# Attention scores on two 64-row halves of the array instead of zero-padded query copies

## The chip, the cores and the metric
The kernel runs on one NeuronCore of a Trainium2 chip. The metric is the device time of one execution in microseconds (us); lower is better.

## The reference
One transformer layer over 1024 tokens of width 1024, all in fp32. Two groups of attention heads work side by side on one input projection; the scores `s` are what the change is about.

```
u = rmsnorm(h, attn_norm_g);  qa, ka, va, qb, kb, vb = split(u @ w_in)
# A: 8 query heads, 2 key/value heads, head width 64; a 64-token chunk of queries
#    reads its own chunk and the one before it (128 keys), with a sink and a T5 bias
s = einsum('bcqhgd,bckhd->bchgqk', qc, kb) / sqrt(64) + bias
m = maximum(max(s), sink);  e = exp(s - m);  w = e / (sum(e) + exp(sink - m));  oA = w @ v
# B: 4 heads, each with two query/key halves t=0,1 of width 64, value width 128
s = einsum('bqhtd,bkhtd->bhtqk', qb, k) / sqrt(64) + bias   # causal by chunks of 64
pr = softmax(s);  a = pr[t=0] - lam * pr[t=1];  oB = rmsnorm(a @ v) * 0.8
h = h + concat(oA, oB) @ w_out
h = h + relu(rmsnorm(h) @ w_up)**2 @ w_down
h = h + sigmoid(rmsnorm(h) @ w_gate) * (p @ w_ple)
y = rmsnorm(h)
```

## The kernel before
Activations lie transposed: features on the 128 partitions, 1024 tokens along the free axis. The large projections split each fp32 factor into a high and a low part and run three passes (`passes`, line 781; `wblock`, line 790). The order on each engine is written out by hand with semaphores.

The input projection makes 18 blocks of 128 features: two for A's keys and values (`KA`, `VA`), four for A's queries (`QA`), and per head of B one each for queries, keys and values (`QB`, `KB`, `VB`). A query block of A holds one query head of the first key/value head on partitions 0 to 63 and one of the second on 64 to 127 (`load_qa`, line 265); the one key block holds both key heads in the same way. A block of B holds t=0 on partitions 0 to 63 and t=1 on 64 to 127.

A score matmul contracts over 64 partitions only. The kernel before gives TensorE all 128: GpSimd copies the 64 rows of queries that count into `qs`, a buffer whose other 64 rows were set to zero once (line 396), and the matmul takes the whole key block as its moving operand. `stage_a` (line 412) makes these copies for A, `stage_b` (line 431) for B; `qs_ok` tells TensorE that they are there, and GpSimd waits on `a_s` before it overwrites one.

**Attention A** runs over eight tiles i of 128 queries. For each group g (one key/value head with its four query heads) TensorE does `score_a(i+1, g)`, `trans_a(i, g)` (transposes of the exponentials), `pv_a` (times the values) and, once a tile, `out_a` (`tile_a`, line 940). VectorE's `tile_a` (line 1326) does `den_a`, `soft_a` (adds the bias, takes the maximum), `norm_a` and `split_a`; ScalarE exponentiates (`exp_a`) and copies the transposes out (`evac_a`). The scores of the first tile are computed inside the block before last of the projection (`first_scores`, line 1021).

**Attention B** runs over 4 heads and, in each, 8 steps k. `ORDER = (0, 7, 1, 6, 2, 5, 3, 4)` gives the query block of a step: odd steps have long key ranges (1024, 896, 768, 640 columns), even steps short ones (128, 256, 384, 512). PSUM holds the scores of two steps. TensorE in step k (line 1003): `score_b(k+2, 0)`, `trans_b(k, 0)`, in steps 3 and 4 `out_b` of the previous head, `score_b(k+2, 1)`, a second round of `trans_b` where the range is over 512 columns, then `pv_b(k-1)`. `trans_b(k)` waits for `mix_b(k)`. VectorE in step k (line 1397): `soft_b(k+1, 1)`, in steps 3 and 4 `head_lo`, `soft_b(k+2, 0)`, `mix_b(k+1)`; `soft_b` adds the bias (L1353) and reduces to the maximum (L1356), `mix_b` joins the exponentials of the two halves (L1366, L1368, L1373) and waits for both. ScalarE in step k (line 655): `evac_b(k, 0)`, in steps 3 and 4 `head_hi` of the previous head, `exp_b(k+1, 1)`, a second `evac_b`, `take_b(k-1)`, `exp_b(k+2, 0)`.

Of the kernel before, what the change touches and what calls it, by code (L numbers as in the profile page):

```python
# [24 lines left out]
P = 128  # L25
T = 1024
# [53 lines left out]
def build(nc, x, p, attn_norm_g, w_in, rel_bias, sinks, lam_q1, lam_k1, lam_q2, lam_k2, subln_g, w_out,  # L80
          mlp_norm_g, w_up, w_down, ple_norm_g, w_gate, w_ple, final_norm_g, onehot, out):
    ctx = ExitStack()
    with ctx:
# [56 lines left out]
        qs = at("qs", [P, 8 * P], F32, a_qs)  # L140
# [38 lines left out]

        def s_at(k, t):  # L180

            return (2 + 2 * t) * 512 if k % 2 else t * 512
# [31 lines left out]
        qs_zero, qs_ok = sem("qs_zero"), sem("qs_ok")  # L214
# [39 lines left out]
        def _(sp):  # L254
# [30 lines left out]
            sp.dma_start(sink[:, :], sinks[0].partition_broadcast(P)).then_inc(misc_in, 16)  # L285
# [19 lines left out]
            for i in range(12):  # L305
                head = line_rows[i * P * LINE:(i + 1) * P * LINE - P].rearrange("(q l) -> q l", l=LINE - 1)
                head = head[:, P - 1:P - 1 + 256]
                dst = bias_a[:, i * 256:(i + 1) * 256] if i < 8 else bias_b[:, (i - 8) * 256:(i - 7) * 256]
# [53 lines left out]
        def _(pool):  # L362
# [32 lines left out]
            pool.wait_ge(x_ss, TT)  # L395
            nc.gpsimd.memset(qs[:, :], 0.0).then_inc(qs_zero, 1)
# [8 lines left out]
            pool.wait_ge(qs_zero, 1)  # L405
            nc.gpsimd.memset(ba[64:128, :, 0:128], NEG).then_inc(bias_ok, 1)
            pool.wait_ge(bias_ok, 4)
            pool.wait_ge(ps_free, QB)
            q3 = qkv[:, :].rearrange("p (j t) -> p j t", t=T)
            qs3 = qs[:, :].rearrange("p (j t) -> p j t", t=P)  # L410
# [12 lines left out]
            stage_a(0, more=False)  # L423
            pool.wait_ge(qs_ok, 2)
# [3 lines left out]
            with pool.Fori(1, TT) as i:  # L428
                stage_a(i)
# [18 lines left out]
            pool.wait_ge(a_s, 2 * TT)  # L448
            pool.wait_ge(ps_free, KB)
            for k in range(4):  # L450
                stage_b(0, k, reuse=False)
            for k in range(4, 8):
                stage_b(0, k)
            pool.wait_ge(qs_ok, AU + 2 * TT)
            for s in range(2):
                split_lo(OUT0 + s, s)
            with pool.Fori(0, B_HEADS - 1) as hh:
                for k in range(6):
                    stage_b(hh + 1, k)
                pool.wait_ge(qs_ok, AU + 2 * TT * (hh + 1) + 12)  # L460
                root_b(hh)
                for k in range(6, 8):
                    stage_b(hh + 1, k)
            pool.wait_ge(qs_ok, AU + 2 * TT * B_HEADS)
            root_b(B_HEADS - 1)
# [314 lines left out]
        def _(pe):  # L780
# [127 lines left out]
            def trans_a(i, g):  # L908
                pe.wait_ge(a_e, 2 * i + g + 1)
                if not (isinstance(i, int) and i == 0 and g == 0):  # L910
                    pe.wait_ge(a_at, 2 * i + g)
# [676 lines left out]
```

## Time and profile before
| | |
|---|---|
| runs | 1382.13, 1383.05, 1386.3 us; median 1383.05 |
| span of the profiled execution, first to last instruction | 1379.7 us |
| TensorE busy | 1333.9 us, 97% |
| VectorE busy | 442.2 us, 32% |
| ScalarE busy | 355.9 us, 26% |
| GpSimd busy | 477.8 us, 35% |
| mean granted TensorE clock | 0.994 |
| input projection | to about 240 us |
| attention A | about 240 to 313 us |
| attention B | about 313 to 457 us |
| output projection, MLP, gate, output | the rest |

The profile names engines PE (TensorE matmul), PEld (its weight loads, which overlap), DVE (VectorE), ACT (ScalarE), POOL (GpSimd) and SP or SPq (SyncE and its queue). "L970" is line 970 of the kernel. An fp32 matmul stands in it as two MATMUL and two LDWEIGHTS records, a transpose or a matmul of the split parts as one each. The end of a matmul is modelled, so records overlap; the time from start to start is what a record costs. All times count from the start of the span.

### The profile page before, as it was taken

The numbers are of one execution on the slowest core, as the hardware profiler recorded it, in microseconds if no ns is written. First come the engines' busy times: TensorE is split into PE (matmuls) and PEld (weight loads), VectorE is DVE, ScalarE is ACT, GpSimd is POOL, SyncE is SP. The second block draws the span as 40 slices with busy tenths as digits, with TensorE's granted clock in tenths as the row PEclk, the third lists the DMA queues.
The fourth block names the chain that finished last, engine by engine and source line by source line (L and its number), as shares of the span: only waits on it lengthen the run. The fifth ranks groups of instructions, "written<-read, shape, count | busy, mean of one in ns | idle before, by whom it ended". The sixth has DMA issues, their size and how long they took to land.

```text
span 1379.7 us, 17463 instructions
## 1 busy us (share of the span) xinstructions
PE 1333.9 (97%) x6285; PEld 1090.7 (79%) x6285; DVE 442.2 (32%) x598; ACT 355.9 (26%) x655; POOL 477.8 (35%) x293
## 2 busy tenths in 40 slices
PE   6999999998888899999999999999999999999997
PEld 5788888995555788888888888888888888888886
DVE  5510112887888232222111221122211122222324
ACT  7112101665666311121011110011100122113221
POOL 3121231112221377433223432234322334774743
PEclk9999999999999999999999999999999999999999
DMA  5433111001000312111111121111121111113203
GB/s 190 173 94 92 46 46 31 0 1 31 1 0 0 138 46 60 32 59 47 46 46 46 47 60 46 46 46 46 46 60 46 46 46 46 48 43 98 70 0 123
DMA packets 117872, 75.38 MB, mean 55 GB/s; under 512 B 12817, under 2 KB 115250, under 8 KB 117458
## 3 DMA queue, kind: packets, MB, share of 16 engines
q1 hardware_dynamic: 117554, 73.93, 17.3%
q10 hardware_dynamic: 288, 1.05, 0.2%
q8 instruction: 19, 0.31, 0.1%
q14 instruction: 11, 0.09, 0.0%
HBM read 64.22 MB, written 10.75 MB: 54 GB/s over the span
## 4 chain that ended last, share of the span: by engine, by line
PE 90%; DVE 3%; ACT 2%; issue 2%; DMA 0%; DVEq 0%; SPq 0%; ACTq 0%
PE ps L787 77%; PE ps L812 3%; PE ps L903 2%; PE ps L928 2%; PE ps L970 2%; ACT e_buf L627 1%; PE ps L990 1%; PE ps L980 1%; PE ps L916 1%; DVE e_buf L1373 1%; PE ps L871 1%; DMA x_raw<-in_x 0%; PE ps L820 0%; PE ps L1072 0%; DVE coef L1368 0%
## 5 line engine op out<-in xcount | busy, mean ns | idle before, releaser
L366 POOL TENSOR_TENSOR w_lo<-w_raw,w_hi 128x1024 fp32r<-128x1024 f32 x96 | 230.9, 2406 | 621.7 <-ACT w_hi L551 621.6
L787 PE MATMUL ps<-u_hi,w_hi 128*128 128x512 f32 x896 | 277.0, 390 | 0.0
L787 PE MATMUL ps<-u_lo,w_hi 128*128 128x512 f32 x896 | 276.1, 389 | 0.0
L787 PE MATMUL ps<-u_hi,w_lo 128*128 128x512 f32 x896 | 275.8, 389 | 0.0
L551 ACT CAST w_hi<-w_raw 128x1024 fp32r<-128x1024 f32 x98 | 103.3, 1054 | 651.9 <-PE ps L787 651.1
L787 PEld LDWEIGHTS ps<-u_hi,w_lo 128*128 128x128 f32 x896 | 168.2, 188 | 35.1
L787 PEld LDWEIGHTS ps<-u_lo,w_hi 128*128 128x128 f32 x896 | 168.2, 188 | 35.1
L787 PEld LDWEIGHTS ps<-u_hi,w_hi 128*128 128x128 f32 x896 | 167.4, 188 | 35.7 <-issue 1.6
L787 PE MATMUL ps<-z_hi,w_hi 128*128 128x512 f32 x624 | 193.4, 391 | 0.0
L787 PE MATMUL ps<-z_hi,w_lo 128*128 128x512 f32 x624 | 192.1, 389 | 0.0
L787 PE MATMUL ps<-z_lo,w_hi 128*128 128x512 f32 x624 | 192.1, 389 | 0.0
L1441 DVE TENSOR_TENSOR h<-ps,h 128x1024 f32 (+1 forms) x40 | 49.0, 1225 | 306.0 <-PE ps L787 306.0
L787 PEld LDWEIGHTS ps<-z_hi,w_hi 128*128 128x128 f32 x624 | 116.8, 188 | 25.3 <-issue 1.0
L787 PEld LDWEIGHTS ps<-z_lo,w_hi 128*128 128x128 f32 x624 | 117.1, 188 | 24.4
L787 PEld LDWEIGHTS ps<-z_hi,w_lo 128*128 128x128 f32 x624 | 117.1, 188 | 24.4
L1479 DVE TENSOR_TENSOR u_lo<-temp,u_hi 128x1024 f32 x32 | 39.2, 1226 | 173.2 <-ACT u_hi L703 170.0
L1476 DVE SCALAR_TENSOR_TENSOR temp<-ps,rstd 128x1024 f32<-128x1024 f32 x32 | 39.2, 1224 | 110.1 <-PE ps L787 106.5
L970 PE MATMUL ps<-qkv,qs 128*128 (+4 forms) x192 | 73.2, 494 | 0.0
L1246 DVE SCALAR_TENSOR_TENSOR qkv<-ps,rstd 128x1024 f32 (+1 forms) x18 | 22.0, 1225 | 152.9 <-PE ps L787 146.2
L703 ACT CAST u_hi<-temp 128x1024 f32 (+1 forms) x31 | 32.5, 1049 | 138.0 <-POOL temp L498 138.0
L473 POOL TENSOR_TENSOR sqt<-h 128x1024 f32 (+1 forms) x23 | 59.3, 2580 | 17.0 <-DVE h L1508 17.0
L498 POOL TENSOR_TENSOR temp<-temp 128x1024 f32<-128x1024 f32 x32 | 60.6, 1893 | 6.0 <-DVE temp L1476 6.0
(149 smaller groups left out, 1227.8 us busy)
## 6 DMA issues: line engine op xcount, KB each, us to landing
w_raw<-in_w_up SPq DMA_DIRECT2D x64, 256.0 KB, 3.0
w_raw<-in_w_down SPq DMA_DIRECT2D x64, 256.0 KB, 3.0
w_raw<-in_w_in SPq DMA_DIRECT2D x36, 256.0 KB, 3.2
x_raw<-in_x SPq DMA_DIRECT2D x8, 512.0 KB, 6.9
h_save<-h SPq DMA_DIRECT2D x1, 4096.0 KB, 11.1
w_raw<-in_w_out SPq DMA_DIRECT2D x16, 256.0 KB, 2.9
w_raw<-in_w_ple_gate SPq DMA_DIRECT2D x16, 256.0 KB, 3.0
out<-y_out SPq DMA_DIRECT2D x6, 512.0 KB, 5.1
```

Source lines behind the costliest of these rows:

```text
L366: nc.gpsimd.tensor_tensor(w_lo[:, s * D:(s + 1) * D], w_raw[:, s * D:(s + 1) * D], w_hi[:, s * D:(s + 1) * D].bitcast(F32), ALU.subtract). ...
L473: nc.gpsimd.tensor_tensor(sqt[:, :], hj, hj, ALU.mult).then_inc(sq_t, 1)
L498: nc.gpsimd.tensor_tensor(tj, tj, tj, ALU.mult).then_inc(z_sq, 1)
L551: nc.scalar.copy(w_hi[:, s * D:(s + 1) * D], w_raw[:, s * D:(s + 1) * D]).then_inc(hi_done, 1)
L703: nc.scalar.copy(u_hi[:, bass.ds((2 * i + s) * T, T)], temp[:, s * T:(s + 1) * T]).then_inc(z_hid, 1)
L787: mm = nc.tensor.matmul(o[i], w, xx[:, x0[i]], start=(first and n == 0), stop=(last and n == 2))
L812: mm = nc.tensor.matmul(bank(2 * s + half), w, xx[:, x0], start=(k == 0 and n == 0), stop=(k == DT - 1 and n == 2))
L903: mm = nc.tensor.matmul(ps[:, g * T + j * 256:g * T + (j + 1) * 256], qs[:, (4 * g + j) * P:(4 * g + j + 1) * P], qkv[:, bass.ds(KA * T + ...
L970: mm = nc.tensor.matmul(ps[:, s0:s0 + w], qs[:, q0:q0 + P], qkv[:, bass.ds((KB + hh) * T + c, w)], start=True, stop=True)
L1441: nc.vector.tensor_tensor(hj, bank(2 * s, 2), hj, ALU.add).then_inc(ps_free, 1)
L1476: nc.vector.scalar_tensor_tensor(out=tj, in0=bank(2 * s, 2), scalar=0.0, in1=rstd[:, :], op0=ALU.max, op1=ALU.mult).then_inc(ps_free, 1)
L1479: nc.vector.tensor_tensor(u_lo[:, bass.ds(j * T, T)], tj, u_hi[:, bass.ds(j * T, T)].bitcast(F32), ALU.subtract).then_inc(z_ok, 1)
```

## The change
The query copies go, with the buffer `qs`, the semaphores `qs_zero` and `qs_ok` and all of GpSimd's `stage_a` and `stage_b`. A score matmul now takes its 64 rows of queries and of keys straight from `qkv`, on partitions 0 to 63 or 64 to 127, so that the two matmuls of a pair use the two halves of the array's rows; they alternate in program order and write different PSUM banks.

In A a group g is now made of two query blocks with both their halves, in place of the four query heads of one key/value head. Sinks and biases are loaded in that order (`a_place`; four DMAs for the sinks in place of one), `pv_a` picks the value head by `j // 2`, and `out_a` puts the heads back in order.

In B `score_b` makes both halves in one call. It waits for the exponentials of both halves of step k-2, and in `step_b` it stands behind `trans_b(hh, k, 0)`, and ahead of `out_b`; before, t=0 stood in front of the transposes and t=1 behind `out_b`. In the last tile of A `score_b(0, 0)` for both halves stands where the t=1 half stood. On VectorE and ScalarE the order stays. TensorE's loops over tiles and heads are unrolled.

```
+        def a_place(head):
+
+            return 4 * (head % 4 // 2) + 2 * (head // 4) + head % 2
...
-            sp.dma_start(sink[:, :], sinks[0].partition_broadcast(P)).then_inc(misc_in, 16)
+            for c in range(4):
+                h0 = 4 * (c % 2) + 2 * (c // 2)
+                sp.dma_start(sink[:, 2 * c:2 * c + 2], sinks[0, h0:h0 + 2].partition_broadcast(P)).then_inc(misc_in, 16)
...
-            nc.gpsimd.memset(qs[:, :], 0.0).then_inc(qs_zero, 1)
...
-            def stage_a(i, more=True):
-
-                for g in range(2):
-                    if more:
-                        pool.wait_ge(a_s, 2 * i - 1 + g)
-                        pool.wait_ge(qs_ok, 2 * i + g)
-                    elif g:
-                        pool.wait_ge(qs_ok, 1)
-                    nc.gpsimd.tensor_copy(qs3[g * HD:(g + 1) * HD, 4 * g:4 * g + 4, :],
-                                          q3[g * HD:(g + 1) * HD, QA:QA + 4, bass.ds(i * P, P)]).then_inc(qs_ok, 1)
-
-            stage_a(0, more=False)
...
-            def stage_b(hh, k, reuse=True):
-
-                u = TT * hh + k
-                if reuse:
-                    pool.wait_ge(a_s, AU + 2 * (u - 4) + 2)
-                for t in range(2):
-                    pool.wait_ge(qs_ok, AU + 2 * u + t)
-                    nc.gpsimd.tensor_copy(qs3[t * HD:(t + 1) * HD, 4 * t + k % 4, :],
-                                          qkv[t * HD:(t + 1) * HD, bass.ds((QB + hh) * T + ORDER[k] * P, P)]
-                                          ).then_inc(qs_ok, 1)
-
...
             def score_a(i, g, k0):
-                pe.wait_ge(qs_ok, 2 * i + g + 1)
-                if not isinstance(i, int) or i > 0:
+                if i > 0:
                     pe.wait_ge(a_e, 2 * (i - 1) + g + 1)
-                for j in range(4):
-                    mm = nc.tensor.matmul(ps[:, g * T + j * 256:g * T + (j + 1) * 256],
-                                          qs[:, (4 * g + j) * P:(4 * g + j + 1) * P],
-                                          qkv[:, bass.ds(KA * T + k0, 256)], start=True, stop=True)
+                for j in range(2):
+                    for r in range(2):
+                        rows = slice(r * HD, (r + 1) * HD)
+                        q0, s0 = (QA + 2 * g + j) * T + i * P, g * T + r * HALF + j * 256
+                        mm = nc.tensor.matmul(ps[:, s0:s0 + 256], qkv[rows, q0:q0 + P],
+                                              qkv[rows, KA * T + k0:KA * T + k0 + 256], start=True, stop=True)
                 mm.then_inc(a_s, 1)
...
-                                              qkv[:, bass.ds(VA * T + k0 + kt * P + g * HD, HD)],
+                                              qkv[:, bass.ds(VA * T + k0 + kt * P + (j // 2) * HD, HD)],
...
-                    mm = nc.tensor.transpose(ps[:, 7 * 512 + j * P:7 * 512 + (j + 1) * P],
-                                             o_a[:, j * P:(j + 1) * P], ident[:, :])
+                    x0 = 7 * 512 + (2 * (j % 2) + j // 2) * P
+                    mm = nc.tensor.transpose(ps[:, x0:x0 + P], o_a[:, j * P:(j + 1) * P], ident[:, :])
...
                 for g in range(2):
                     if ahead:
                         score_a(i + 1, g, k1)
-                    else:
-                        score_b(0, 0, g)
+                    elif g:
+                        score_b(0, 0)
                     trans_a(i, g)
...
-            def score_b(hh, k, t):
+            def score_b(hh, k):
 
                 u = TT * hh + k
                 n = (ORDER[k] + 1) * P
-                pe.wait_ge(qs_ok, AU + 2 * u + t + 1)
-                if isinstance(hh, int) and hh == 0 and k < 2:
-                    pe.wait_ge(a_e, 2 * TT - 1 + k)
+                if u < 2:
+                    pe.wait_ge(a_e, 2 * TT)
                     if k:
                         pe.wait_ge(a_at, 2 * TT)
                 else:
-                    pe.wait_ge(a_e, AU + 2 * (u - 2) + t + 1)
+                    pe.wait_ge(a_e, AU + 2 * (u - 2) + 2)
                 for c in range(0, n, HALF):
                     w = min(HALF, n - c)
-                    q0, s0 = (4 * t + k % 4) * P, s_at(k, t) + c
-                    mm = nc.tensor.matmul(ps[:, s0:s0 + w], qs[:, q0:q0 + P],
-                                          qkv[:, bass.ds((KB + hh) * T + c, w)], start=True, stop=True)
-                mm.then_inc(a_s, 1)
+                    for t in range(2):
+                        rows = slice(t * HD, (t + 1) * HD)
+                        q0, k0, s0 = (QB + hh) * T + ORDER[k] * P, (KB + hh) * T + c, s_at(k, t) + c
+                        mm = nc.tensor.matmul(ps[:, s0:s0 + w], qkv[rows, q0:q0 + P], qkv[rows, k0:k0 + w],
+                                              start=True, stop=True)
+                        if c + w == n:
+                            mm.then_inc(a_s, 1)
...
             def step_b(hh, k, ahead=True, prev=None):
                 h2, k2 = (hh, k + 2) if k < 6 else (hh + 1, k - 6)
+                trans_b(hh, k, 0)
                 if ahead:
-                    score_b(h2, k2, 0)
-                trans_b(hh, k, 0)
+                    score_b(h2, k2)
                 if prev is not None and k >= 3:
                     pe.wait_ge(b_oc, TT * hh + k - 1)
                     out_b(prev, k - 3)
-                if ahead:
-                    score_b(h2, k2, 1)
                 if ROUNDS[k] == 2:
                     trans_b(hh, k, 1)
                 if prev is not None and k >= 3:
...
-            with pe.Fori(2, TT - 1) as i:
+            for i in range(2, TT - 1):
                 tile_a(i, (i - 2) * P, (i - 1) * P, i * P)
...
-            for t in range(2):
-                score_b(0, 1, t)
+            score_b(0, 1)
...
-            with pe.Fori(0, B_HEADS - 1) as hh:
+            for hh in range(B_HEADS - 1):
                 for k in range(SPLIT, TT):
```

## Rows read from the trace of the kernel before
**Rows 1.** The page's head: span, and each engine's busy time, share, instructions.

```profile
span 1379.7 us, 17463 instructions
PE 1333.9 (97%) x6285; PEld 1090.7 (79%) x6285; DVE 442.2 (32%) x598; ACT 355.9 (26%) x655; POOL 477.8 (35%) x293
```

**Rows 2.** Busy time by stretch, columns as in the header: A tile, B head.

```profile
254.21:263.42 9.21, 9.21 (x70) 8.70 (x70) 8.09 (x17) 6.07 (x21) 1.22 (x2) 1.00 0.00 0
349.85:385.00 35.15, 30.24 (x167) 20.39 (x166) 29.45 (x61) 23.92 (x70) 7.57 (x17) 1.00 0.00 0
```

**Rows 3.** Waits, 241 to 303 us: who for whom, us in total, times, longest.

```profile
DVE ps L1284 <- PE ps L903: 5.0, 8, 0.8
```

**Rows 4.** The chain that ended last: start us, length us, what.

```profile
217.18 3.45 PE ps L903 x16
...
265.16 1.78 PE ps L903 x8
...
380.99 1.72 PE ps L970 x4
```

**Rows 5.** Waits of one head of B, 349.85 to 385 us.

```profile
DVE rden L1366 <- ACT e_buf L627: 2.9, 3, 1.6
```

**Rows 6.** Timeline around the 32-row matmuls: start us, length us, what.

```profile
55.05 0.61 PE L787 MATMUL ps<-u_hi,w_lo 128*128 128x512 f32 x2
...
55.59 2.84 PE L871 MATMUL ps<-hotw,ones 32*128 32x384 f32 x8
...
58.36 0.72 PE L787 MATMUL ps<-u_hi,w_hi 128*128 128x512 f32 x2
```

**Rows 7.** Timeline, end of A, VectorE.

```profile
305.94 0.42 DVE L1305 TENSOR_TENSOR o_a<-ps,rden 128x256 f32<-128x256 f32 x1 [1.35 <-PE ps L928]
```

**Rows 8.** Timeline around k=7 of a head of B.

```profile
381.50 0.89 DVE L1373 SCALAR_TENSOR_TENSOR e_buf<-e_buf,coef 128x640 f32<-128x640 f32 x1
...
382.54 0.63 PE L980 MATMUL ps<-ident,e_buf 128*128 128x128 f32 x4
...
382.86 0.43 DVE L1353 TENSOR_TENSOR ps<-ps,bias_b 128x256 f32<-128x256 f32 x1
...
383.01 1.88 PE L970 MATMUL ps<-qkv,qs 128*128 x4
...
385.64 1.22 DVE L1356 TENSOR_REDUCE nmax<-ps 128x1 f32<-128x1024 f32 x1
...
387.86 1.14 ACT L627 ACTIVATE e_buf<-ps,nmax 128x1024 f32<-128x1024 f32 x1
...
389.21 0.17 DVE L1366 RECIPROCAL rden<-den_t 128x2 f32<-128x2 f32 x1 [1.55 <-ACT e_buf L627]
```

**Rows 9.** Timeline behind k=1.

```profile
355.94 0.65 PE L980 MATMUL ps<-ident,e_buf 128*128 128x128 f32 x4 [1.34 <-DVE e_buf L1373]
...
356.52 0.42 DVE L1353 TENSOR_TENSOR ps<-ps,bias_b 128x256 f32<-128x256 f32 x1
```

**Rows 10.** Timeline behind k=5, VectorE.

```profile
374.04 1.02 DVE L1373 SCALAR_TENSOR_TENSOR e_buf<-e_buf,coef 128x768 f32<-128x768 f32 x1
...
376.04 0.42 DVE L1353 TENSOR_TENSOR ps<-ps,bias_b 128x256 f32<-128x256 f32 x1
```

**Rows 11.** Timeline behind k=3, the previous head's output.

```profile
365.08 0.63 PE L999 MATMUL ps<-ident,o_n 128*128 128x128 f32 x4 [0.59 <-DVE o_n L1385]
...
366.71 0.75 DVE L1393 SCALAR_TENSOR_TENSOR u_lo<-ps,gb,u_hi 128x512 f32 x1 [0.84 <-ACT u_hi L652]
```

**Rows 12.** SyncE's DMA issues around its gap.

```profile
12.52 0.43 SPq L287 DMA_DIRECT2D lam_in<-in_lam_k  x1
...
18.52 4.32 SPq L263 DMA_DIRECT2D w_raw<-in_w_in  x4
```

**Rows 13.** Busy time and granted clock (the number behind POOL) by stretch.

```profile
308.90:310.60 1.70, 1.09 (x10) 0.98 (x10) 0.47 (x2) 0.00 (x0) 0.00 (x0) 1.00 0.00 0
...
312.30:314.00 1.70, 1.68 (x5) 1.25 (x6) 0.53 (x1) 0.00 (x0) 0.00 (x0) 0.50 0.00 0
```

More of the change, by code:

```diff
@@ L139, in build @@
         diag = at("diag", [P, TT * P], F32, a_rstd)
-        qs = at("qs", [P, 8 * P], F32, a_qs)
         def small(name, n, parts=P):
@@ L213, in build @@
         v_tr, v_cp = sem("v_tr"), sem("v_cp")
-        qs_zero, qs_ok = sem("qs_zero"), sem("qs_ok")
         a_s, a_m, a_e = sem("a_s"), sem("a_m"), sem("a_e")
@@ L307, in _ @@
                 head = head[:, P - 1:P - 1 + 256]
-                dst = bias_a[:, i * 256:(i + 1) * 256] if i < 8 else bias_b[:, (i - 8) * 256:(i - 7) * 256]
+                at_a = a_place(i) if i < 8 else 0
+                dst = bias_a[:, at_a * 256:(at_a + 1) * 256] if i < 8 else bias_b[:, (i - 8) * 256:(i - 7) * 256]
                 sp.dma_start(dst, head).then_inc(bias_in, 16)
@@ L393, in _ @@
                     split_lo(2 * i + s, s)
-            pool.wait_ge(x_ss, TT)
-            nc.gpsimd.memset(qs[:, :], 0.0).then_inc(qs_zero, 1)
             pool.wait_ge(bias_in, 12 * 16)
@@ L404, in _ @@
             pool.wait_ge(bias_ok, 3)
-            pool.wait_ge(qs_zero, 1)
             nc.gpsimd.memset(ba[64:128, :, 0:128], NEG).then_inc(bias_ok, 1)
             pool.wait_ge(bias_ok, 4)
-            pool.wait_ge(ps_free, QB)
-            q3 = qkv[:, :].rearrange("p (j t) -> p j t", t=T)
-            qs3 = qs[:, :].rearrange("p (j t) -> p j t", t=P)
-            def stage_a(i, more=True):
-                for g in range(2):
-                    if more:
-                        pool.wait_ge(a_s, 2 * i - 1 + g)
-                        pool.wait_ge(qs_ok, 2 * i + g)
-                    elif g:
-                        pool.wait_ge(qs_ok, 1)
-                    nc.gpsimd.tensor_copy(qs3[g * HD:(g + 1) * HD, 4 * g:4 * g + 4, :],
-                                          q3[g * HD:(g + 1) * HD, QA:QA + 4, bass.ds(i * P, P)]).then_inc(qs_ok, 1)
-            stage_a(0, more=False)
-            pool.wait_ge(qs_ok, 2)
             with pool.Fori(KB // 2, N_IN // 2) as i:
@@ L427, in _ @@
                     split_lo(2 * i + s, s)
-            with pool.Fori(1, TT) as i:
-                stage_a(i)
-            def stage_b(hh, k, reuse=True):
-                u = TT * hh + k
-                if reuse:
-                    pool.wait_ge(a_s, AU + 2 * (u - 4) + 2)
-                for t in range(2):
-                    pool.wait_ge(qs_ok, AU + 2 * u + t)
-                    nc.gpsimd.tensor_copy(qs3[t * HD:(t + 1) * HD, 4 * t + k % 4, :],
-                                          qkv[t * HD:(t + 1) * HD, bass.ds((QB + hh) * T + ORDER[k] * P, P)]
-                                          ).then_inc(qs_ok, 1)
             def root_b(hh):
@@ L446, in root_b @@
                 pool.wait_ge(b_rt, hh + 1)
[L448 to L454, printed above, removed]
             for s in range(2):
                 split_lo(OUT0 + s, s)
[L457 to L460, printed above, removed]
+            with pool.Fori(0, B_HEADS) as hh:
                 root_b(hh)
[L462 to L465, printed above, removed]
             def square(b, j, n, clears):
@@ L909, in trans_a @@
                 pe.wait_ge(a_e, 2 * i + g + 1)
-                if not (isinstance(i, int) and i == 0 and g == 0):
+                if i or g:
                     pe.wait_ge(a_at, 2 * i + g)
@@ L920, in pv_a @@
                 pe.wait_ge(a_at, 2 * i + g + 1)
-                if isinstance(i, int) and i == 0 and g == 0:
+                if i == 0 and g == 0:
                     pe.wait_ge(ps_free, N_IN)
@@ L1209, in _ @@
                 if t == 6:
-                    dve.wait_ge(misc_in, 7 * 16)
+                    dve.wait_ge(misc_in, 10 * 16)
                     l4 = lam_in[:, :].rearrange("p (a b d) -> p a b d", b=2, d=HD)
```

## Prediction, made before the changed kernel was run

> **What bounds the kernel now.** I began with the page [rows 1]: the span is 1379.7 us and TensorE is busy for 97% of it. Most of that is the projection and MLP blocks of line 787, which the change leaves alone. The score matmuls run only between 217 and 455 us, so the busy share of the whole says nothing here, and I asked next for the busy time in stretches of that part [rows 2]. In one tile of attention A (9.21 us) TensorE is busy throughout and VectorE for 8.09 us: TensorE is the bound, VectorE close behind. In one head of attention B (35.15 us) neither is full: TensorE 30.24 us, VectorE 29.45 us. There the order of the work decides, and the question for each edit is who waits for whom.
>
> The waits in A [rows 3] show VectorE waiting for the scores of line 903, 8 times, 5.0 us in total. That is all VectorE can win back. The chain of waits [rows 4] gives the price of the scores: each fp32 matmul leaves two records, and a record takes 3.45/16 = 0.216 us at 256 columns and 1.72/4 = 0.43 us at 512. In B the waits of VectorE [rows 5] go above all to the exponentials (2.9 us a head); none is for scores. Its idle time there is not caused by the length of a score matmul, since `score_b(k+2, 0)` was issued ahead of `trans_b(k, 0)`, in time in which TensorE waits for `mix_b(k)` anyway.
>
> **The change part by part.**
> *What a pair costs.* I take it that matmuls start in program order, that the two records of one matmul use the same half of the array and so follow each other, and that the first record for the other half may run beside the second. With a record D, two pairs of A then take 5 D instead of 8 D: 1.08 us instead of 1.73. In B the half t=0 is ready after as many records as before (its own), and t=1 one record later. No run here shows two halves side by side. The bounds are 4 D (full overlap) and 8 D (none); I take 5 D because the trace has the matmuls of a group strictly one behind the other at D [rows 4].
>
> The Trainium skill's "TensorE: Matmul & The Clock Gate" (Part 3, Packing small matmuls) has matmuls of different row groups starting some nanoseconds apart. Nothing in this trace shows it. By it a pair would take 2 D, and the result would be some 3 us lower than mine.
>
> *Going to a part of the array and back.* The nearest rows are the 32-row matmuls of line 871 [rows 6]. From the start of the first to the next full matmul lie 58.36 - 55.59 = 2.77 us for 8 records of 384 columns, where streaming at 0.43 x 384/512 = 0.32 us makes 2.58. The last full pair before starts at 55.05, 0.54 us ahead of the visit; its two records last 0.61 us with their tail and would be followed after an estimated 0.45. So a switch costs 0.1 us or so each way. Bounds: 0 and 0.3 us. It comes twice for every group of scores.
>
> Those rows show a small gap at each side of the visit. The Trainium skill's "TensorEngine Tiling (Array Packing)" (Tiling Modes, Key Properties) says that changing the mode drains the engine, which speaks against a change that alternates modes in each step; the trace agrees, at 0.1 us. Without it the sum would be 2.4 us smaller.
>
> *First scores.* 16 records of 0.216 become 9 of them plus two switches: 3.45 -> 1.94 + 0.2, -1.3 us. TensorE is busy before and after them, so all of it counts.
>
> *Tiles of A.* TensorE falls by 6 D = 1.3 us a tile and gains 4 switches (0.4): 9.2 -> 8.3 us. VectorE needs 9.21 less its wait, 8.5, and is next. So the gain is the 5.0 us of [rows 3], not the 7 that TensorE saves.
>
> *From A to B.* `score_b(0, 0)` now stands behind `pv_a(6, 1)` for both halves; VectorE wants its t=0 half ahead of `norm_a(6, 1)`, which it now starts at 305.94 [rows 7]. It waits for the scores (0.3) and adds and reduces them (0.6) first; 0.5 us of this is time that the next link waits for `trans_a` anyway. +0.4, between 0 and 0.9.
>
> *B: where the t=0 scores went.* Both halves now follow `trans_b(k, 0)`, which waits for `mix_b(k)`. VectorE's order is unchanged: after `mix_b(k)` it takes `soft_b(k+1, 1)`, then `soft_b(k+2, 0)`, then `mix_b(k+1)`. For odd k the next key range is long (1024, 896, 768, 640) and the work that covers it, `soft_b(k+1, 1)`, is short. Take k=7 [rows 8]: `mix_b` ends at 382.39, `trans_b` starts at 382.54 and the scores behind it at 383.01. The half t=0 (1024 columns, 4 records) is ready at 384.73, while VectorE began `soft_b` on it at 382.86, from scores made earlier. With 0.1 of hand-off it waits 1.95 us. Part comes back: the `mix_b` at 389.21 waited 1.55 us for exponentials that began at 387.86, though their `soft_b` was through at 385.64 + 1.22 = 386.86, because ScalarE's queue was behind. Now that `soft_b` is through at 388.8, the exponentials run from 388.95 for 1.35 us, and `mix_b` follows at 390.3 instead of 389.21. Net +1.1, 3 times.
> - k=1 (896 columns, records 2 x 0.43 + 2 x 0.32) [rows 9]: `trans_b` starts at 355.94, its scores 0.47 later, t=0 is ready at 357.9 plus 0.1; VectorE used it at 356.52. It waits 1.5 us and gets 0.3 back at the next exponential: +1.2 three times, +0.85 in head 0, 4.45 in all.
> - k=5 (640 columns, records 2 x 0.43 + 2 x 0.11) [rows 10]: `mix_b` ends at 375.06, and by the same steps the scores are ready 0.15 + 0.45 + 1.1 + 0.1 = 1.8 us later, where VectorE took them up at 376.04, after 1.0: +0.75, 4 times.
> - k=3 and k=4 with a previous head [rows 11]: `out_b` stood between the two halves, now behind both. For k=3 it goes from 365.08 to 366.1 (768 columns, the whole pair), for k=4 the full 3 D = 1.3 us comes ahead of it. VectorE's `head_lo` waits for `out_b` through ScalarE (366.71 against 365.08), so it slips by +1.0 and +1.3, 3 times each. In head 0 k=3 has no `out_b`, but its own late scores: +0.9.
> - Even k: the next range is short and `soft_b(k+1, 1)` long (1.2 us and more), so the scores are in time: 0.
>
> Sum: 3.3 + 4.45 + 3.0 + 3.0 + 3.9 + 0.9 = 18.55 us, and switches ahead of these 18 crossings (1.8) and behind the six with `out_b` (0.6): 21.0 us.
>
> *The rest.* GpSimd's copies into `qs` go: they were ahead of the scores, and no score waited for them. Three more DMA issues for `sink` fall in SyncE's gap from 12.95 to 18.52 us [rows 12], at 0.43 to 0.47 us each; if that gap were gone they would cost 1.4 us. The unrolled loops of TensorE cost nothing that a row shows: bounds -0.3 (fewer register operations, off the path) and +2 us (waiting for code, one long wait of this size); I take 0, as the unrolled head 0 runs like the looped ones.
>
> **Sum.** -1.3 - 5.0 + 0.4 + 21.0 = +15.1 us. Against the profiled execution's span this is 1394.8. The median of the runs, 1383.05, lies 3.35 us above that span, for what is outside the first and last instruction, so I predict 1383.05 + 15 = 1398 us.
>
> **The rivals.**
> - *TensorE bounds B as well, and the shorter scores pay.* For: it is the busiest engine and 90% of the chain that ended last. Against: [rows 5]. A head would save D for the four short ranges (1.1 us) and 0.43 + 2 D' for the long ones, D' being the second record (3.85): 4.9 us, 19.7 in four heads, with 5.9 in A: -25.6, 1357 us. It decides if VectorE's next instruction after `soft_b(k+1, 1)` does not wait for the scores, or if later waits give the delay back in full.
> - *No overlap (the change doesn't do what it says).* A saves nothing; t=0 is ready two records later in 15 crossings (0.86 each) and `out_b` one record later in three: 12.9 + 1.3. 15.1 + 5.9 + 14.2 = +35, 1418 us. For: fp32 matmuls of the same group never overlap now. Against: here the rows used are disjoint.
> - *The clock falls.* TensorE's granted clock was 1.00 all through B, but it fell to 0.50 (1.2 of 2.4 GHz) at 312.3 us, where shortly before it had been busy for 1.09 of 1.70 us [rows 13]. With the change B has TensorE busy about 60% of the time. About 9 us a head of transposes and scores lie on the path; at half clock for a third of B this is +12: 1410 us.
> - *The delays are mostly absorbed.* If ScalarE's and TensorE's slack returns more than I traced, B costs half, 10 us: 1387 us.
>
> **How the numbers follow.** Forecast 0.55, no overlap 0.10, clock 0.12, absorbed 0.10, TensorE bound 0.13. The range 1384 to 1418 takes in all but the TensorE-bound case and some tail: the low end is B at half cost with full overlap, the high end the case without overlap. A measurement here can tell about 0.3%, 4 us, from no change. Faster 0.14, same 0.08, slower 0.78.
>
> **What would show it.** In the new trace: VectorE's `soft_b` adds waiting 1 to 2 us for TensorE's scores behind odd k, about four times a head; a head lasting 40 us; a tile of A 8.5 us with VectorE full; first scores 2 us. A head under 35 us would make the order argument wrong; scores of 1024 columns lasting 3.4 us for both halves would mean no overlap; a granted clock below 0.9 in B would be the third rival.

## The result: 1408.8 us, and the profile of the changed kernel

| | before | changed |
|---|---|---|
| runs | 1382.1 to 1386.3 us | 1404.16, 1405.36, 1412.31, 1412.56 us |
| median | 1383.2 us | 1408.8 us |
| ratio of times | | 1.018 (95%: 1.015 to 1.021) |
| profiled run, its span | span 1379.7 us | 1412.31 us, span 1410.5 us |

The changed kernel is 1.8% slower; 1398 us was forecast, and the median lies inside the range of 1384 to 1418. Its runs fall in two pairs, and the mean granted clock goes with them: 0.978 in the two of 1404 and 1405 us, 0.970 in the two of 1412 us.

The head of the page, to be held against [rows 1]:

```profile
span 1410.5 us, 16954 instructions
PE 1332.0 (94%) x6285; PEld 1080.7 (77%) x6285; DVE 441.9 (31%) x598; ACT 355.6 (25%) x655; POOL 445.4 (32%) x212
...
PEclk8999999999788799999999999999999999999999
```

TensorE's busy time has hardly moved (1333.9 to 1332.0 us) though its score matmuls got shorter: a lower clock has stretched others. The row of the clock has its dip in slices 11 to 14 (353 to 494 us), which are most of attention B and a few us behind it.

I cut both profiled executions at the same places: the first record of the first scores, of A, of B, and of the output projection.

| stretch, us | before | changed | difference | forecast |
|---|---|---|---|---|
| up to the first scores | 217.2 | 218.8 | +1.6 | 0 |
| first scores to A | 22.35 | 21.17 | -1.2 | -1.3 |
| A with the hand-over to B | 73.7 | 68.1 | -5.6 | -4.6 |
| B | 143.8 | 178.3 | +34.5 | +21.0 |
| the rest | 922.6 | 924.2 | +1.5 | 0 |
| span | 1379.7 | 1410.5 | +30.8 | +15.1 |

The 1.6 us ahead of the first scores are not the change's doing: in the profiled executions of the experiments this stretch took 216 to 219 us, and 217 us in experiment 1, whose code is the same up to there.

Busy time by stretch of the changed kernel: all of A, all of B, one tile of A, one head of B, and the stretch behind the first scores of B. The columns are the stretch, its length, then busy time and instructions of PE, PEld, DVE, ACT and POOL, then the granted clock and DMA.

```profile
239.97:308.04 68.07, 64.77 (x534) 56.55 (x533) 59.58 (x123) 43.88 (x146) 0.00 (x0) 1.00 0.00 1
308.04:486.33 178.29, 122.57 (x646) 80.53 (x645) 116.77 (x234) 95.78 (x273) 9.78 (x5) 0.83 0.04 13
247.99:256.43 8.44, 8.44 (x73) 7.56 (x72) 8.02 (x18) 7.31 (x28) 0.00 (x0) 1.00 0.01 2
411.64:456.71 45.07, 31.90 (x164) 20.93 (x164) 29.56 (x61) 24.03 (x71) 1.64 (x1) 0.81 0.00 1
312.00:316.00 4.00, 1.60 (x5) 0.69 (x5) 3.45 (x9) 3.16 (x8) 0.00 (x0) 0.51 0.00 0
```

A tile of A takes 8.44 us against 9.21 [rows 2]. In the head of B VectorE's work is the same as before (29.56 us) and the head is 10 us longer, with a granted clock of 0.81 where before it was 1.00.

The waits of the whole attention part, 217 to 490 us (engine and line that wait, for whom, us in total, times, longest):

```profile
PE ps L940 <- DVE e_buf L1330: 41.1, 27, 3.0
...
DVE ps L1310 <- PE ps L929: 31.6, 16, 3.7
...
DVE u_lo L1350 <- ACT u_hi L609: 16.4, 6, 3.7
```

Line 929 is the score matmul of B, line 1310 VectorE's first add on scores (`soft_b`), line 940 the transposes, line 1350 `head_lo`. Before, VectorE waited in B mostly for exponentials [rows 5], and for scores once in all of B, 1.4 us; now it waits for scores 15 times in B and once (2.3 us) at the end of A. TensorE's waits for `mix_b` were 16.6 us in 17 times before and are 41.1 us in 27 now. The chain of waits shows the shorter pairs, to be held against [rows 4]; the `x8` row of line 929 is a whole pair of 1024 columns:

```profile
218.80 1.93 PE ps L862 x16
...
391.97 1.97 PE ps L929 x8
```

And the timeline behind k=7, the counterpart of [rows 8]:

```profile
391.32 0.66 PE L940 MATMUL ps<-ident,e_buf 128*128 128x128 f32 x4 [0.97 <-DVE e_buf L1330]
...
391.90 1.99 PE L929 MATMUL ps<-qkv 64*128 64x512 f32 x8
...
394.03 0.43 DVE L1310 TENSOR_TENSOR ps<-ps,bias_b 128x256 f32<-128x256 f32 x1 [2.23 <-PE ps L929]
```

The transposes wait for `mix_b` (e_buf, L1330), the scores stand behind them, and VectorE is idle for 2.23 us before its add; 1.95 us was forecast.

So the order theory has its mark in the trace, but B lost 13.5 us more than that theory forecast. Two things were to be told apart: the new places of the scores, and TensorE's clock.

### The profile page after: what moved, and what is told of

The parts are those of the page before. It is cut to its first block, busy times and chain, and to the rows that moved or that the text cites. A ratio compares the mean times of both kernels' runs of the same rounds, so it can differ in the third digit from the quotient of the medians.

```text
span 1410.5 us, 16954 instructions
## 1 busy us (share of the span) xinstructions
PE 1332.0 (94%) x6285; PEld 1080.7 (77%) x6285; DVE 441.9 (31%) x598; ACT 355.6 (25%) x655; POOL 445.4 (32%) x212
## 4 chain that ended last, share of the span: by engine, by line
PE 87%; DVE 7%; issue 2%; ACT 1%; DMA 1%; SPq 0%; DVEq 0%; ACTq 0%
PE ps L744 75%; PE ps L929 3%; PE ps L769 2%; PE ps L950 1%; PE ps L940 1%; DVE e_buf L1330 1%; DVE kmax L1244 1%; DVE ps L1241 1%; ACT e_buf L584 1%; DMA x_raw<-in_x 1%; DVE ps L1310 1%; PE ps L828 1%; DVE nmax L1313 0%; DVE coef L1325 0%; PE ps L959 0%
## 5 line engine op out<-in xcount | busy, mean ns | idle before, releaser
L744 PEld LDWEIGHTS ps<-u_hi,w_lo 128*128 128x128 f32 x896 | 169.0, 189 | 35.4
L940 PE MATMUL ps<-ident,e_buf 128*128 128x128 f32 x144 | 30.0, 326 | 45.0 <-DVE e_buf L1330 41.1
L940 PEld LDWEIGHTS ps<-ident,e_buf 128*128 128x128 f32 x144 | 18.6, 162 | 58.7 <-DVE e_buf L1330 46.8
```

What stands on the lines that cost most here:

```text
L744: mm = nc.tensor.matmul(o[i], w, xx[:, x0[i]], start=(first and n == 0), stop=(last and n == 2))
L940: mm = nc.tensor.transpose(ps[:, o:o + P], e_buf[:, e:e + P], ident[:, :])
```

## The experiments

All medians below stand against runs of the kernel before on the same chip (medians 1381.9 to 1383.2 us). The granted clock of B and B's length are from each kernel's own profiled execution.

### 1. Only the order put back: the pair ahead of the transposes

```
             def step_b(hh, k, ahead=True, prev=None):
-                trans_b(hh, k, 0)
                 if ahead:
                     score_b(h2, k2)
+                trans_b(hh, k, 0)
```

> The changed kernel with one edit: in each step of B both halves of score_b(k+2) stand ahead of trans_b(k, 0) instead of behind it. Order theory (the loss in B is VectorE waiting for the late t=0 scores and the late out_b): these waits go, B returns to the 144 us it had before or a little less, A keeps its 7 us; 1373 to 1382 us, and VectorE's adds of line 1310 wait under 5 us in all instead of 31.6. Rival, 64-row matmuls or the switches between array modes are what costs: the time stays above 1395 us. Rival, the clock: if TensorE's clock falls because 64-row matmuls count for less, it still falls here and the time lies between, near 1390 us.

Measured: 1380.9 us, ratio 1.0003 (0.998 to 1.003). One line moved gives back 28 us. B takes 145.7 us at a clock of 0.95 (the changed kernel's 178.3 at 0.83), so the 28 us are the order and what the clock lost with it. VectorE's waits for scores fall from 31.6 us to 5.6 (under 5 was expected), and the longest of them is at the end of A:

```profile
DVE ps L1310 <- PE ps L929: 5.6, 7, 2.8
```

Two middle heads read:

```profile
356.80:391.22 34.42, 25.66 (x166) 17.19 (x164) 29.36 (x61) 23.71 (x70) 1.64 (x1) 1.00 0.00 0
391.22:427.24 36.02, 27.27 (x166) 18.35 (x164) 29.47 (x61) 23.71 (x70) 1.64 (x1) 0.95 0.00 0
```

At full clock a head is 0.7 us shorter than before (35.15 [rows 2]), though TensorE has 4.6 us less to do in it: shorter scores are worth little in B. The next head has the same work at a clock of 0.95 and takes 1.6 us longer, so what was won goes again.

### 2. Only the places, without 64-row matmuls

The kernel before, with both calls moved to where the changed kernel has its pair.

```
+                trans_b(hh, k, 0)
                 if ahead:
                     score_b(h2, k2, 0)
-                trans_b(hh, k, 0)
+                    score_b(h2, k2, 1)
                 if prev is not None and k >= 3:
                     pe.wait_ge(b_oc, TT * hh + k - 1)
                     out_b(prev, k - 3)
-                if ahead:
-                    score_b(h2, k2, 1)
```

> The kernel before, zero-padded copies and all 128 rows, with one edit: both score_b calls of a step of B stand behind trans_b(k, 0) and ahead of out_b, as in the changed kernel. Order theory: B loses what the changed kernel lost there and some more, as the pair takes 8 D instead of 5 D ahead of out_b; A is as before: 1405 to 1418 us. Rivals (64 rows, mode switches): 1383 to 1388 us, no change.

Measured: 1418.0 us, ratio 1.026 (1.023 to 1.029). B takes 179.2 us, 35.4 more than before, with the padded copies and full-height matmuls all in place:

```profile
313.26:492.49 179.23, 131.29 (x646) 89.63 (x645) 117.62 (x234) 94.22 (x273) 32.17 (x59) 0.94 0.04 12
```

The places alone slow B down; the halves of the array are not needed for that. VectorE now waits for the padded scores too (300 to 490 us), and no wait of TensorE for GpSimd's copies shows there:

```profile
DVE ps L1352 <- PE ps L970: 23.4, 14, 3.2
```

The clock here is 0.94, so a part of the 35 us is clock too.

### 3. Only the halves, in the old places

The changed kernel, with `score_b(hh, k, t)` one half at a time where the kernel before had it (also at the end of A).

```
+                if ahead:
+                    score_b(h2, k2, 0)
                 trans_b(hh, k, 0)
-                if ahead:
-                    score_b(h2, k2)
                 if prev is not None and k >= 3:
                     pe.wait_ge(b_oc, TT * hh + k - 1)
                     out_b(prev, k - 3)
+                if ahead:
+                    score_b(h2, k2, 1)
```

> The changed kernel with the halves taken from 64 rows, but each score_b in its old place in B (t=0 ahead of the transposes, t=1 behind out_b, also at the end of A), so that pairs do not overlap in B and the array changes its mode twice as often. Order theory: B as before, A as in the changed kernel; 1375 to 1380 us. Mode-switch rival: two more switches a step, 32 steps, at 0.1 us or more each on the path: 1385 us or more. 64-row rival: above 1395 us.

Measured: 1388.9 us, ratio 1.005 (1.003 to 1.007); a miss, 9 us over the upper end of the order theory; the rival of the mode switches, 1385 us or more, had it right. A middle head:

```profile
368.81:405.34 36.53, 34.57 (x165) 20.89 (x164) 29.54 (x62) 23.93 (x72) 1.64 (x1) 1.00 0.00 0
```

At the same full clock a head is 1.4 us longer than before and TensorE is busy 4.3 us more, in 16 visits to one half of the array: 0.27 us a visit. Unpaired, they pay for going there and back and save nothing. All of B takes 159.5 us, TensorE is busy for 146.1 of them, a larger share than before, and yet the clock is 0.91; that was the first sign that the busy share alone doesn't tell the clock. The two middle heads both ran at 1.00, so the 1.4 us a head are not clock; the low stretches lie in the first head (0.51 from 318 to 335 us) and at the end of B.

### 4. The pair on one half: is there overlap?

```
                     for t in range(2):
-                        rows = slice(t * HD, (t + 1) * HD)
+                        rows = slice(0, HD)
```

and the same in `score_a`.

> The changed kernel with both matmuls of every pair on rows 0 to 63 (the scores of the second half are then computed from the first half's queries and keys, so that part of the result is left out). If the two halves of the array really run side by side, this takes it away: 16 first-score records take 3.45 us instead of 1.93, a tile of A 9.2 us instead of 8.4, long ranges of B are ready 0.5 to 0.9 us later: 1420 to 1430 us. If nothing overlapped, the time stays at 1405 to 1412 us.

Measured: 1462.8 us, ratio 1.058 (1.055 to 1.061). The size was missed by over 30 us. The first scores:

```profile
216.79 3.65 PE ps L862 x16
```

3.65 us against 1.93 for the same 16 records on alternating halves, whose streaming alone would be 3.45 one behind the other and 1.73 side by side: they do overlap, and fully. B takes 215.6 us, and this is why the size was missed:

```profile
318.42:534.03 215.61, 178.80 (x646) 110.43 (x645) 116.88 (x234) 95.36 (x273) 9.79 (x5) 0.73 0.03 8
```

TensorE is busy for 83% of B, about as in the kernel before (120.6 of 143.8 us, 84%, clock 0.99), and is granted 0.73. The two shares are not quite alike: at a lower clock the same matmuls stay busy longer, so a part of the 83% comes from the low clock itself.

### 5 and 6. Holding the clock: an idle matmul ahead of each wait for `mix_b`

```
+                pe.wait_ge(a_at, AU + HEAD_ROUNDS * hh + BEFORE[k] + r)
+                if r == 0:
+                    nc.tensor.matmul(ps[:, 6 * 512:6 * 512 + 512], ident[:, :], qkv[:, KA * T:KA * T + 512],
+                                     start=True, stop=True)
                 pe.wait_ge(b_a, TT * hh + k + 1)
-                pe.wait_ge(a_at, AU + HEAD_ROUNDS * hh + BEFORE[k] + r)
```

This adds work to the changed kernel (32 matmuls whose result nobody reads); to free their PSUM bank, the wait for `a_at` moves ahead of the wait for `mix_b`, which is alike in both kernels. In the second kernel they use rows 0 to 63 only (`ident[0:64, :]`, `qkv[0:64, ...]`), with the same columns.

> The changed kernel plus one idle matmul in each step of B: 128 rows, 512 fp32 columns into the transposes' bank, while TensorE waits for mix_b ahead of trans_b(k, 0); its result is overwritten. 32 of them, 0.86 us each, 27.5 us of extra TensorE work, part of it past the end of the wait. Clock theory (beyond the 20 us of the late scores, B loses some 5 to 15 us because the granted clock falls to 0.8): the clock in B rises above 0.93 and the time falls in spite of the extra work, to 1395 to 1403 us. Rival, order alone: the clock is no cause, the extra work costs where it overruns, 1409 to 1425 us.

> The same with the idle matmul on 64 of the 128 rows. If TensorE's clock is held up by the matmuls' being there, this does as well as the 128-row one, within 3 us. If 64-row matmuls hold the clock up less, the granted clock in B stays nearer to the changed kernel's 0.83 and the time lies 4 us or more above that of the 128-row one.

Measured: 1399.2 us (ratio 1.011, 1.008 to 1.013) with all 128 rows, 1410.8 us (1.020, 1.018 to 1.023) with 64. B, first with 128 rows and below it a head of it:

```profile
309.84:476.20 166.36, 135.47 (x709) 77.99 (x709) 116.67 (x234) 96.24 (x273) 9.78 (x5) 0.97 0.04 10
409.94:450.27 40.33, 32.80 (x180) 19.07 (x180) 29.54 (x61) 24.15 (x71) 1.64 (x1) 1.00 0.00 0
```

and with 64 rows:

```profile
309.60:485.15 175.55, 148.56 (x709) 85.03 (x709) 116.75 (x234) 96.42 (x273) 9.78 (x5) 0.90 0.04 14
```

Added work makes the kernel 9.6 us faster (8.4 us when each is held against the kernel before of its own session): the clock in B goes from 0.83 to 0.97. So the third rival, the clock, was at work beside the forecast. At full clock the head takes 40.3 us, the 40 us that the order argument gave; it holds eight idle matmuls, and what these add to it was not measured. With 64 rows the same columns gain nothing in the median and the clock stays at 0.90, although by the records TensorE was busy longer. The moved wait is in both kernels, so it is not what gained. A part of the 11.6 us between the two can be the visits to 64 rows rather than the clock: at the 0.3 us a visit worked out below, 32 of them are an estimated 10 us, less what falls into waits.

### 7. Only A and the first scores changed

B as before: `qs`, `stage_b` and the padded `score_b(hh, k, t)` in their old places; A as in the changed kernel.

```
                     if ahead:
                         score_a(i + 1, g, k1)
-                    elif g:
-                        score_b(0, 0)
+                    else:
+                        score_b(0, 0, g)
...
-                        mm = nc.tensor.matmul(ps[:, s0:s0 + w], qkv[rows, q0:q0 + P], qkv[rows, k0:k0 + w],
...
+                    mm = nc.tensor.matmul(ps[:, s0:s0 + w], qs[:, q0:q0 + P],
+                                          qkv[:, bass.ds((KB + hh) * T + c, w)], start=True, stop=True)
```

> The change in A alone (two halves of the array, new head order), B as in the kernel before with zero-padded copies, its old places and all rows. Order theory: first scores and A give 7 us, B stays at 144 us: 1375 to 1378 us. Against the kernel with 64 rows and the old places (1388.9 us), this tells what 64-row scores cost in B: if they cost nothing there, both would be equal and this one would come at 1388 us too.

Measured: 1378.9 us, ratio 0.997 (0.995 to 0.998), 3 us faster than before, and 0.9 us over the expected range. Middle heads of B last 35.14 us as before; 1388 us, which would have meant that 64-row scores cost nothing in B, did not come. The clock ate part of the gain at the end of A:

```profile
306.00:310.00 4.00, 3.48 (x12) 2.58 (x12) 1.54 (x3) 0.00 (x0) 0.00 (x0) 0.50 0.00 0
```

A takes 70.2 us here, at 0.95, against 68.1 at 1.00 in the changed kernel's profiled execution, and B 145.9 us at 0.98.

### 8. The pair ahead of the transposes, and idle matmuls

Experiment 1 with the idle matmul of experiment 5, at 256 columns, in each step.

> The kernel with the pair ahead of the transposes (1380.9 us, runs from 1378 to 1390 us with the granted clock between 0.989 and 0.974) plus one idle matmul of 128 rows and 256 columns in each step of B, in the wait ahead of trans_b(k, 0). Clock theory: the spread closes and the median falls to 1372 to 1378 us. Rival: the spread has another cause, the 32 x 0.43 us cost where they overrun: 1381 to 1390 us.

Measured: 1381.5 us, ratio 0.999 (0.998 to 1.001): nothing gained, and 3.5 us over the range that the clock theory gave; the spread stayed too (1374.4 to 1386.5 us). The middle heads take 35.30 us at clock 1.00, against 34.42 in experiment 1: the idle matmuls cost 0.9 us a head. B's clock is 0.97 against 0.95.

### 9. The halves in the old places, and idle matmuls

Experiment 3 with the same idle matmul of 256 columns.

> The kernel with 64-row scores in their old places (1388.9 us, B 159.5 us at a granted clock of 0.91) plus one idle matmul of 128 rows and 256 columns in each step of B ahead of trans_b(k, 0). Clock theory (what that kernel loses in B against the 144 us of the kernel before is the clock): clock in B above 0.96, B 146 to 152 us, 1377 to 1384 us. Rival, the 64-row records and mode switches themselves cost it: the time stays at 1388 us or rises by the filler, up to 1400 us.

Measured: 1396.2 us, ratio 1.011 (1.008 to 1.015), slower than without, and not the 1377 to 1384 us of the clock theory; the rival was right. The clock in B rises from 0.91 to 0.97, but TensorE is now busy for 38.2 of the 38.9 us of a head: where it had no time to spare, the idle matmul is work.

### 10. Idle matmuls only in the gaps at the end of A and the start of B

Experiment 7 with seven idle matmuls in all (`fill(b, n)`: n columns into bank b).

```
                     elif prev:
+                        if not ahead:
+                            fill(1, 256)
                         pv_a(i - 1, 1, km)
...
+                pe.wait_ge(a_at, AU + HEAD_ROUNDS * hh + BEFORE[k] + r)
+                if isinstance(hh, int) and hh == 0 and r == 0 and k in (1, 3):
+                    for _ in range(2):
+                        fill(6, 512)
                 pe.wait_ge(b_a, TT * hh + k + 1)
-                pe.wait_ge(a_at, AU + HEAD_ROUNDS * hh + BEFORE[k] + r)
...
+            fill(2, 384)
             pv_a(TT - 1, 1, (TT - 2) * P)
+            fill(2, 384)
             out_a(TT - 1)
```

> The kernel with A changed and B old (1378.85 us) plus seven idle matmuls between A and B: 256 and 384 columns in the waits of the last tile of A for norm_a, two of 512 columns each ahead of the first waits for mix_b in steps 1 and 3 of head 0. Clock theory: the granted clock no longer falls to 0.50 between 297 and 312 us, 1373 to 1377 us. Rival: the fall has another cause and the fillers only delay: 1379 to 1383 us.

Measured: 1374.2 us (1373.7 to 1375.9), ratio 0.994 (0.992 to 0.996): faster than both kernels. The stretch shown for experiment 7 now runs at full clock:

```profile
306.00:310.00 4.00, 3.44 (x12) 1.81 (x11) 3.56 (x8) 1.47 (x3) 0.58 (x2) 1.00 0.00 0
```

A takes 67.4 us (73.7 before), B 144.0, as before.

### 11. `out_b` ahead of the pair

Experiment 5 (clock held), with one more thing put back: the previous head's output ahead of the scores.

```
                 trans_b(hh, k, 0)
-                if ahead:
-                    score_b(h2, k2)
                 if prev is not None and k >= 3:
                     pe.wait_ge(b_oc, TT * hh + k - 1)
                     out_b(prev, k - 3)
+                if ahead:
+                    score_b(h2, k2)
```

> The changed kernel with the 128-row idle matmuls of 512 columns (1399.2 us, a head 40.3 us at full clock) and one more edit: out_b stands ahead of score_b(k+2), so that the previous head's output no longer waits for the pair; the scores of all steps stay behind trans_b(k, 0). The prediction put 2.3 us a head on this, the rest on the late t=0 scores. If so: a head of 38 us, 1391 to 1394 us, and VectorE's waits for scores keep their 5 to 8 us a head. Rival, the late scores are all of it: no change, 1398 to 1401 us, as u_lo then only waits elsewhere.

Measured: 1391.3 us, ratio 1.006 (1.004 to 1.008). A head:

```profile
405.36:443.62 38.26, 32.95 (x180) 19.15 (x180) 29.56 (x62) 24.27 (x71) 1.64 (x1) 1.00 0.00 1
```

38.26 us against 40.33, both at clock 1.00: 2.1 us a head come from `out_b`, where the prediction had 2.3 plus 0.2 for switches. VectorE's waits for scores are the same in both heads, 4.9 us in 3, so the late scores are the rest.

### 12. Experiment 1 with few idle matmuls

Those of experiment 10, and one of 512 columns in step 3 of the later heads.

> The kernel with the pair ahead of the transposes (1380.9 us; a head 34.4 us where the clock was 1.00, against 35.1 before) with idle matmuls only where TensorE waits long: the same between A and B as in the best kernel so far (1374.2 us), and 512 columns ahead of trans_b in step 3 of each head. Clock theory: clock at 0.99, the spread below 4 us, heads of 34.4 to 35 us, 1371 to 1375 us. Rival, this order needs a filler in every step: the spread stays 8 us or more, median 1377 us or more.

Measured: 1379.7 us, ratio 0.998 (0.997 to 0.999); 1371 to 1375 was expected, and the rival's 1377 or more came, without its spread. The runs draw together (a spread of 2.5 us where experiment 1 had 12) and the middle heads hold 34.40 us at 1.00, but B's clock is still 0.96 over all, with stretches at 0.50 around 314 and 450 us. Where else idle matmuls would have to stand for it was not tried.

## Why the prediction came out as it did

**The median and the range.** The median lies 10.8 us above the 1398 us and inside the range, and that is partly luck. The upper end, 1418, was worked out for halves that do not overlap. They overlap in full; what filled the gap was the clock, which the sum had at nothing.

**First scores and A: right.** 1.2 us for 1.3, and 5.6 with the hand-over for 4.6. The tile is bound by VectorE as forecast: it is busy for 8.02 of 8.44 us, and from 256 to 273 us the chain of waits holds no instruction of TensorE, where before (254 to 273 us) it held nothing else. TensorE's 8.44 busy us in the tile are no sign against it, since the ends of its records are modelled. The hand-over's late scores are there:

```profile
300.95 0.30 DVE L1310 TENSOR_TENSOR ps<-ps,bias_b 128x128 f32<-128x128 f32 x1 [2.29 <-PE ps L929]
...
301.50 0.41 DVE L1262 TENSOR_TENSOR o_a<-ps,rden 128x256 f32<-128x256 f32 x1
```

From one `norm_a` to the next there are now 3.53 us (297.97 to 301.50) where there were 2.57 (303.37 to 305.94 [rows 7]); from that one to the one after, 2.90 (301.50 to 304.40) where there were 3.32 (305.94 to 309.26). That is +1.0 and -0.4, so +0.5 for the forecast +0.4, and the tiles gave about 6 us for 5.0.

**What a pair costs: wrong in form, near in sum.** I took 5 records for two pairs because fp32 records of one half follow each other, and 0.1 us for each switch. Sixteen records take 1.93 us, which is 8 x 0.216 = 1.73 and 0.2 besides. From start to start the pair behind k=7 takes 1.92 us:

```profile
393.82 0.33 PE L940 MATMUL ps<-ident,e_buf 128*128 128x128 f32 x1
```

1.92 is 4 x 0.43 = 1.72 and 0.2 again. The four transposes ahead of it take 0.58 us (391.32 to 391.90) where they took 0.47 (382.54 to 383.01 [rows 8]), 0.1 more. So the two halves overlap in full, and a visit costs 0.1 us going in and 0.2 going back, 0.3 where 0.2 was forecast. The pair was priced one record (0.2 to 0.4 us) too dear, so the two nearly cancel; in experiment 3 the visit shows by itself (0.27 us). The Trainium skill's "TensorE: Matmul & The Clock Gate" (Part 3, Packing small matmuls), which has matmuls of different row groups running side by side, is borne out by the 1.93 against 3.65 us of experiment 4, better than my 5 records. The draining on a change of mode in the Trainium skill's "TensorEngine Tiling (Array Packing)" (Tiling Modes, Key Properties) fits the 0.3 us a visit, though no run shows what those 0.3 us consist of.

**Where the scores stand in B: right.** The k=7 wait was 2.23 us for 1.95. At full clock (experiment 5) the three waits of VectorE for scores in a head are those forecast: k=7 2.23 us, and behind k=1 and k=5

```profile
443.64 0.43 DVE L1313 TENSOR_TENSOR ps<-ps,bias_b 128x256 f32<-128x256 f32 x1 [1.65 <-PE ps L929]
...
425.34 0.43 DVE L1313 TENSOR_TENSOR ps<-ps,bias_b 128x256 f32<-128x256 f32 x1 [0.98 <-PE ps L929]
```

1.65 us for 1.5 and 0.98 for 0.8. The head is 5.2 us longer than before, against 5.35 and some 0.6 of switches in the sum; how much of the 5.2 is the idle matmuls is not known. `out_b` was right by experiment 11, and experiments 1 and 2 show the cause from both sides: the pair moved back recovers it, the places alone bring it. All of B with the clock at 0.97 is +22.5 us, its idle matmuls included, for a forecast of +21.0, and the whole kernel is then 1399 us.

**The clock: the step that failed.** I gave the fall of the clock 0.12 as a case of its own, +12 us, and the forecast had it at nothing. The sign that I had named for it, a clock below 0.9 in B, came: 0.83. Between the two levels of 1.00 and 0.50 that is a third of B at half clock, the share the rival's 12 us had assumed. It was not an alternative but in good part a consequence: the same reordering that makes VectorE wait for TensorE also makes TensorE wait for `mix_b` longer (16.6 to 41.1 us). With the one line moved back the clock in B is 0.95, with the reordering alone and full-height matmuls 0.94, with the halves alone in the old places 0.91, and with both 0.83; so the 64-row scores have a part in it as well. The head shown in the section on the result (411.64 to 456.71 us) shows what the clock does to a wait. Behind k=1, at half clock:

```profile
446.68 3.36 PE L929 MATMUL ps<-qkv 64*128 64x512 f32 x8
...
450.08 0.43 DVE L1310 TENSOR_TENSOR ps<-ps,bias_b 128x256 f32<-128x256 f32 x1 [3.69 <-PE ps L929]
```

The pair of 896 columns takes 3.36 us and the wait is 3.69, where at full clock it was 1.65. B's 34.5 us in the profiled run are 22.5 with the clock held at 0.97 and 12 more. Since the idle matmuls themselves may cost something, 12 is an estimate from below of what the clock took there. With the 1.6 us ahead of the first scores, which are not the change's, and 1.5 behind B (the first 10 us there run at 0.84, before at 1.00) this makes up most of the miss of the span. In the medians it is 1408.8 against 1399.2, 8 to 10 us. The other cases fall: no overlap (experiment 4 shows that there is), TensorE as the bound of B (experiment 1: a head gains 0.7 us, not 4.9), mostly absorbed (experiment 11 beside 5, and VectorE's waits at full clock, are as long as forecast). The unrolled loops, which I took at nothing, are all in experiment 1, and it is back at the time of the kernel before.

**A slip in the sum.** I laid the 3.35 us between the median and the profiled span on what lies outside the first and last instruction. In the runs of the changed kernel that is 1.8 us (1412.31 - 1410.5), in those of the kernel before 1.8 to 3.5; so up to 1.5 us of the 3.35 can be that the profiled execution of before was faster than the median. It changes nothing in the argument.

**What stays open.** In these runs 64-row matmuls went with a lower clock than full-height ones: experiment 6 (0.90) beside 5 (0.97), experiment 3 (146.1 of 159.5 us busy, 0.91) beside 2 (131.3 of 179.2 us, 0.94) and 7 (123.0 of 145.9 us, 0.98), and experiment 4. But the middle heads of experiment 3 held 1.00 with them, and what the chip counts was not measured. Experiment 2's own split of its 35 us into order and clock is open too. Nor is it known why experiment 1 loses clock in a later head while the one before it, with the same work, does not.

## What to carry to other kernels

Before shortening an operation, ask where in program order its result is wanted: a pair fused for the array's sake takes the place of its later half, and if that lies behind a wait, the consumer inherits the wait; moving one line was worth 28 us here, four times the 6.8 us that first scores and A won. An edit that made TensorE wait more was paid twice here, by the wait and by the clock, so ask of both together and not as rivals; idle full-height matmuls ahead of the waits told them apart in one run, and a handful of them in real gaps (1378.9 to 1374.2 us) can be worth keeping. Take such a change apart by stage: here only its half in A pays.

## What the hardware showed that I had not expected

- fp32 matmuls on the two 64-row halves overlap in full, both records of each: 1.93 us for 16 records of 256 columns, 3.65 when all use one half.
- One visit to the halves of the array and back costs about 0.3 us beyond the streaming for a pair of eight records (0.1 going in, 0.2 going back), and 0.27 us on average for a single matmul.
- The granted clock did not go by TensorE's busy share alone: full-height scores gave 0.99 in B at 84% busy (before) and 0.94 at 73% (experiment 2), 64-row scores 0.91 at 92% (experiment 3) and 0.73 at 83% (experiment 4). The same 512 idle columns gave 0.97 with 128 rows and 0.90 with 64.
- Added TensorE work that nobody reads made the kernel faster: 1408.8 to 1399.2 us with 32 idle matmuls, 1378.9 to 1374.2 with seven.
